# A fused two-block layer on one core: the y branch's units in halves of 256 features, with both parts of x in one moving operand

## The reference, cut to what matters

```python
h = rmsnorm(x, norm_mix_pre[l])
proj = h @ w_in[l]
xr, yr, q, k, v, g_rnn, g_attn = jnp.split(proj, IN_OFFSETS, axis=-1)
xr = causal_depthwise_conv(xr, conv_w[l], conv_b[l])
xr = rg_lru(xr, positions, w_rg_a[l], b_rg_a[l], w_rg_x[l], b_rg_x[l], lru_lambda[l])
y_rnn = xr * jax.nn.gelu(yr)
...
mix = jax.nn.sigmoid(g_rnn) * (y_rnn @ w_rnn_proj[l]) + jax.nn.sigmoid(g_attn) * (y_att @ w_attn_proj[l])
```

## Time and profile before

| | us |
|---|---|
| median of 3 runs | 2270.91 |
| lowest and highest | 2269.68 and 2271.86 |
| the profiled execution | 2270.5 |
| its span in the profile | 2268.8 |
| PE busy | 2250.7 (99% of the span) |
| DVE busy | 1420.2 (63%) |
| ACT busy | 1221.7 (54%) |
| POOL busy | 349.9 (15%) |

### The profile page before, as it was taken

How to read it: one execution, slowest core, us unless ns; L and a number is a source line. 1 busy time by engine, 2 the same in 40 slices (tenths; PEclk the granted TensorE clock), 3 DMA queues, 4 the chain that set the end, 5 groups by cost and what they waited for, 6 DMA issues and landing times.

```text
span 2268.8 us, 32847 instructions
## 1 busy us (share of the span) xinstructions
PE 2250.7 (99%) x11837; PEld 1896.5 (84%) x11837; DVE 1420.2 (63%) x1633; ACT 1221.7 (54%) x1915; POOL 349.9 (15%) x383
## 2 busy tenths in 40 slices
PE   9999999999999999999999999999999999999999
PEld 7888999888888888888888888889977778888887
DVE  6666656655454575555555555566899967765554
ACT  6666677544444456555555655555444446654443
POOL 2232210000000102121212112120333311110000
PEclk9999999999999999999999999999999999999999
DMA  7454454565555756566666666665556655555654
GB/s 240 151 168 149 148 180 145 195 194 192 192 190 194 244 193 211 197 208 196 203 205 199 201 203 201 195 208 180 177 182 195 191 172 171 166 161 187 192 187 167
DMA packets 215348, 427.10 MB, mean 188 GB/s; under 512 B 14096, under 2 KB 14384, under 8 KB 214960
## 3 DMA queue, kind: packets, MB, share of 16 engines
q1 hardware_dynamic: 206960, 398.57, 55.4%
q0 software_dynamic: 8048, 26.62, 3.8%
q10 hardware_dynamic: 208, 0.07, 0.0%
HBM read 414.71 MB, written 10.49 MB: 187 GB/s over the span
## 4 chain that ended last, share of the span: by engine, by line
PE 81%; DVE 12%; issue 3%; ACT 3%; POOL 1%; DMA 0%; DVEq 0%; ACTq 0%; SPq 0%
PE acc L1983 23%; PE acc L1985 23%; PE acc L1984 23%; DVE w_lo L1193 4%; PE acc L1975 3%; PE acc L1977 3%; PE acc L1978 3%; PE tps L1998 1%; ACT w_hi L674 1%; POOL k_t L589 1%; PE sides L2075 1%; POOL tmp L589 1%; PE tps L2093 1%; DVE slab_f_f L1755 1%; DVE k_t L1749 1%
## 5 line engine op out<-in xcount | busy, mean ns | idle before, releaser
L1193 DVE TENSOR_TENSOR w_lo<-raw,w_hi 128x1024 fp32r<-128x1024 f32 x752 | 942.8, 1258 | 752.4 <-ACT w_hi L674 748.3
L674 ACT ACTIVATE w_hi<-raw 128x1024 fp32r<-128x1024 f32 x752 | 794.7, 1059 | 848.9 <-PE acc L1985 733.4
L1983 PE MATMUL acc<-w_hi,h_hi 128*128 128x512 f32 x1440 | 571.5, 397 | 2.6 <-DVE w_lo L1193 1.7
L1985 PE MATMUL acc<-w_hi,h_lo 128*128 128x512 f32 x1440 | 561.8, 390 | 0.0
L1984 PE MATMUL acc<-w_lo,h_hi 128*128 128x512 f32 x1440 | 561.0, 390 | 0.0
L1983 PEld LDWEIGHTS acc<-w_hi,h_hi 128*128 128x128 f32 x1440 | 270.4, 188 | 68.2 <-issue 15.0
L1985 PEld LDWEIGHTS acc<-w_hi,h_lo 128*128 128x128 f32 x1440 | 270.3, 188 | 57.5
L1984 PEld LDWEIGHTS acc<-w_lo,h_hi 128*128 128x128 f32 x1440 | 270.8, 188 | 53.1
L1983 PE MATMUL acc<-w_hi,slab_dg_r 128*128 128x512 f32 x756 | 294.8, 390 | 0.0
L1985 PE MATMUL acc<-w_hi,slab_dg_r 128*128 128x512 f32 x756 | 294.3, 389 | 0.0
L1984 PE MATMUL acc<-w_lo,slab_dg_r 128*128 128x512 f32 x756 | 294.3, 389 | 0.0
(11 more groups left out here) (391 smaller groups left out, 2332.2 us busy)
## 6 DMA issues: line engine op xcount, KB each, us to landing
raw<-in_w_in_dram SPq DMA_DIRECT2D x328, 512.0 KB, 4.0
raw<-in_w_mlp_up_dram SPq DMA_DIRECT2D x128, 512.0 KB, 3.9
raw<-in_w_mlp_down_dram SPq DMA_DIRECT2D x128, 512.0 KB, 4.0
raw<-in_w_out_dram SPq DMA_DIRECT2D x64, 512.0 KB, 4.2
raw<-in_w_rnn_proj_dram SPq DMA_DIRECT2D x32, 512.0 KB, 3.8
raw<-in_w_attn_proj_dram SPq DMA_DIRECT2D x32, 512.0 KB, 3.8
trig_scratch<-tmp POOLq DMA_DIRECT2D x32, 256.0 KB, 3.8
raw<-in_w_proj_ssm_dram SPq DMA_DIRECT2D x16, 512.0 KB, 3.7
```

Source lines behind the costliest of these rows:

```text
L674: nc.scalar.activation(w_hi[:, j % RING], raw[:, j % RING], ACT.Copy).then_inc(hi_ready, 1)
L1193: V.tensor_tensor(w_lo[:, j % RING], raw[:, j % RING], w_hi[:, j % RING].bitcast(F32), ALU.subtract)\
L1983: T.matmul(o, hi[:, k, c], wh, start=first, stop=False)
L1985: ins = T.matmul(o, lo[:, k, c], wh, start=False, stop=last)
```

## The change

It touches the four y units only.

- SP loads, for each step, 4 k tiles by 256 columns in place of 2 k tiles by 512 (still 512 KB, in rows of 1 KB in place of 2 KB). Steps 0 to 3 of a unit make its first 256 features (half 0), steps 4 to 7 the second (half 1).
- `h_hi` and `h_lo` lie in one tensor `h_both`, so that one moving operand takes both: 256 columns of the high part and 256 of the low part. For each k tile and group of 128 features PE runs one matmul of 512 columns (stationary high weights) and one of 256 (stationary low weights), in place of three of 256.
- Half 0 uses `acc[1]`, half 1 `acc[0]`, in every unit. Each holds two sums per feature, a left one and a right one, which have to be added.
- Evacuation: ACT copies the right sums of a half (512 columns) into `yr_c` (`yr_right`); DVE adds the left sums and then multiplies by the row in a second instruction (`yr_half`, 2 of 512 columns). Half 0 is evacuated in the hooks of step 4 of its own unit, half 1 in the hooks of step 0 of the next.
- gelu moves on ACT from step 0 to step 1, ahead of the gates, and waits for the DVE instructions of half 1.

```diff
-                places = {0: [lambda: gelu(c)], 1: [lambda: gates(c)], 2: [lambda: decays(c)], 4: [lambda: root(c)]}
+                places = {0: [lambda: yr_right(c, 1)], 1: [lambda: gelu(c), lambda: gates(c)], 2: [lambda: decays(c)],
+                          4: [lambda: root(c)]}
...
+            def yr_right(c, h):
+                act.wait_ge(pe_used, (U_YR + c) * S + 4 * h + 4)
...
+                bank = acc[(U_YR + h) % 2][:, :].rearrange("p (m w c) -> p m w c", m=2, w=2)
+                nc.scalar.activation(yr_c[c % 2][:, 2 * h:2 * h + 2, :], bank[:, :, 1, :], ACT.Copy).then_inc(right_ready, 1)
...
+                hooks[4] = [lambda c=c: yr_right(c, 0)] + hooks.get(4, [])
...
+                return {0: [lambda: yr_half(c, 1)], 3: [lambda: decay(c)], 5: [lambda: states(c)], 6: [lambda: y_product(c)],
+                        7: [lambda: y_low(c)]}
+
+            def yr_half(c, h):
...
+                dve.wait_ge(right_ready, 2 * c + h + 1)
+                V.tensor_tensor(out_, left, out_, ALU.add).then_inc(done, 1)
+                dve.wait_ge(done, value)
+                V.tensor_tensor(out_, out_, row[:, :].unsqueeze(1).broadcast_to([P, 2, SEQ]), ALU.mult).then_inc(yr_ready, 1)
...
-                unit_over(None, 0, u * S)
-                rows_ = row[:, :].unsqueeze(1).broadcast_to([P, QPC, SEQ])
-                V.tensor_tensor(yr_c[c % 2], feat(acc[u % 2]), rows_, ALU.mult).then_inc(acc_free[u % 2], 1)
+                hooks = dict(beside_recurrence(c - 1) if c else beside_yr)
+                hooks[4] = hooks.get(4, []) + [lambda c=c: yr_half(c, 0)]
...
+                    for e in range(4):
+                        k = 4 * q + e
+                        for m in range(2):
+                            o = acc[par][:, m * NC:(m + 1) * NC]
+                            T.matmul(o.rearrange("p (w c) -> p w c", w=2), wh[:, e, m * P:(m + 1) * P], h_both[:, :, k, :],
+                                     start=k == 0, stop=False, skip_group_check=True)
+                            ins = T.matmul(o[:, 0:SEQ], wl[:, e, m * P:(m + 1) * P], h_hi[:, k, :], start=False, stop=k == KT - 1,
+                                           skip_group_check=True)
```

More of the change, by code:

```diff
@@ L116, in griffin_block_then_ssm_block @@
         w_lo = sb("w_lo", [P, RING, 2, NC], F32R)
-        h_hi = sb("h_hi", [P, KT, SEQ], F32R)
-        h_lo = sb("h_lo", [P, KT, SEQ], F32R)
+        h_both = sb("h_both", [P, 2, KT, SEQ], F32R)
+        h_hi, h_lo = h_both[:, 0, :, :], h_both[:, 1, :, :]
         slab_dg, slab_dgr = two_views("slab_dg", [P, 2 * KT, SEQ])
@@ L241, in griffin_block_then_ssm_block @@
         x_half_lo = sem("x_half_lo")
+        half_free, yr_ready = [sem(f"half_free{h}") for h in range(2)], sem("yr_ready")
+        right_ready = sem("right_ready")
         x_first, acc_half, sq_part = sem("x_first"), sem("acc_half"), sem("sq_part")
@@ L361, in griffin_block_then_ssm_block, with narrow @@
         row = t_low
+        def narrow(slot):
+            return slot.rearrange("p e (h n) -> p (e h) n", h=2)
         block = ctx.enter_context(nc.Block())
@@ L413, in _ @@
                 for j in range(2):
-                    unit(w_in, ds(past(i, 2 * NC, o_yr + j * NC), NC), past(i, 2 * S, (U_YR + j) * S))
+                    for s in range(S):
+                        sp.wait_ge(lo_ready, past(i, 2 * S, (U_YR + j) * S + s - LEAD))
+                        col = ds(past(i, 2 * NC, o_yr + j * NC + s // 4 * SEQ), SEQ)
+                        sp.dma_start(narrow(raw[:, s % RING, :, :]), w_in[s % 4 * 4 * P:(s % 4 + 1) * 4 * P, col]
+                                     .rearrange("(t p) n -> p t n", p=P)).then_inc(raw_landed[s % RING], 16)
             with sp.Fori(1, NH + 1) as i:
@@ L868, in gelu @@
             def gelu(c):
-                u = U_YR + c
-                act.wait_ge(acc_free[u % 2], u // 2 + 1)
+                act.wait_ge(yr_ready, 2 * c + 2)
                 nc.scalar.activation(yr_c[c % 2], yr_c[c % 2], ACT.Gelu_apprx_tanh).then_inc(gelu_ready, 1)
             def beside_recurrence(c):
-                places = {0: [lambda: gelu(c)], 1: [lambda: gates(c)], 2: [lambda: decays(c)], 4: [lambda: root(c)]}
+                places = {0: [lambda: yr_right(c, 1)], 1: [lambda: gelu(c), lambda: gates(c)], 2: [lambda: decays(c)],
+                          4: [lambda: root(c)]}
                 if c < NH - 1:
@@ L877, in beside_recurrence @@
                 return places
+            def yr_right(c, h):
+                act.wait_ge(pe_used, (U_YR + c) * S + 4 * h + 4)
+                if c == 0:
+                    act.wait_ge(tps_free, T_QX + NH)
+                if c > 1 and h == 0:
+                    act.wait_ge(y_ready, 2 * c - 2)
+                bank = acc[(U_YR + h) % 2][:, :].rearrange("p (m w c) -> p m w c", m=2, w=2)
+                nc.scalar.activation(yr_c[c % 2][:, 2 * h:2 * h + 2, :], bank[:, :, 1, :], ACT.Copy).then_inc(right_ready, 1)
             for c in range(NH):
-                u = U_YR + c
-                steps(None, 0, u * S, beside_recurrence(c - 1) if c else beside_yr)
+                hooks = dict(beside_recurrence(c - 1) if c else beside_yr)
+                hooks[4] = [lambda c=c: yr_right(c, 0)] + hooks.get(4, [])
+                steps(None, 0, (U_YR + c) * S, hooks)
             def mix_unit(i, c, n, hooks=None):
@@ L1470, in beside_recurrence @@
                 if c == NH - 1:
-                    return {3: [lambda: decay(c)], 5: [lambda: states(c)], 6: [lambda: scans(c)], 7: [lambda: y_product(c)]}
-                return {3: [lambda: decay(c)], 5: [lambda: states(c)], 6: [lambda: y_product(c)], 7: [lambda: y_low(c)]}
-            for c in range(NH):
[L1475 to L1478, removed]
-                unit_over(None, 0, u * S)
-                rows_ = row[:, :].unsqueeze(1).broadcast_to([P, QPC, SEQ])
-                V.tensor_tensor(yr_c[c % 2], feat(acc[u % 2]), rows_, ALU.mult).then_inc(acc_free[u % 2], 1)
+                    return {0: [lambda: yr_half(c, 1)], 3: [lambda: decay(c)], 5: [lambda: states(c)], 6: [lambda: scans(c)], 7: [lambda: y_product(c)]}
+                return {0: [lambda: yr_half(c, 1)], 3: [lambda: decay(c)], 5: [lambda: states(c)], 6: [lambda: y_product(c)],
+                        7: [lambda: y_low(c)]}
+            def yr_half(c, h):
+                par = (U_YR + h) % 2
+                out_ = yr_c[c % 2][:, 2 * h:2 * h + 2, :]
+                left = acc[par][:, :].rearrange("p (m w c) -> p m w c", m=2, w=2)[:, :, 0, :]
+                done, value = (half_free[h], c + 1) if c < 2 else (acc_free[par], (U_YR + h) // 2 + c - 1)
+                dve.wait_ge(right_ready, 2 * c + h + 1)
+                V.tensor_tensor(out_, left, out_, ALU.add).then_inc(done, 1)
+                dve.wait_ge(done, value)
+                V.tensor_tensor(out_, out_, row[:, :].unsqueeze(1).broadcast_to([P, 2, SEQ]), ALU.mult).then_inc(yr_ready, 1)
+            for c in range(NH):
+                hooks = dict(beside_recurrence(c - 1) if c else beside_yr)
+                hooks[4] = hooks.get(4, []) + [lambda c=c: yr_half(c, 0)]
+                steps(None, 0, (U_YR + c) * S, hooks)
             def mix_unit(i, c, n, hooks=None):
@@ L2129, in rg, with yr_unit @@
                 ins.then_inc(rg_done, 1)
+            def yr_unit(c, hooks):
+                for s in range(S):
+                    h, q = divmod(s, 4)
+                    par = (U_YR + h) % 2
+                    if q == 0:
+                        if c in (1, 2):
+                            pe.wait_ge(half_free[h], c)
+                        else:
+                            pe.wait_ge(acc_free[par], (U_YR + h) // 2 + c // 3)
+                    pe.wait_ge(lo_ready, (U_YR + c) * S + s + 1)
+                    wh, wl = narrow(w_hi[:, s % RING, :, :]), narrow(w_lo[:, s % RING, :, :])
+                    for e in range(4):
[6 more added lines that the diff above has]
+                                           skip_group_check=True)
+                        if e == 3:
+                            ins.then_inc(pe_used, 1)
+                        if e % 2:
+                            for f in hooks.get(2 * s + e // 2, []):
+                                f()
             for c in range(NH):
-                unit(None, 0, (U_YR + c) * S, 0, U_YR + c, h_hi, h_lo, by_feature=True,
-                     hooks={1: [lambda: rg(c - 1)]} if c else beside_yr)
+                yr_unit(c, {1: [lambda: rg(c - 1)]} if c else beside_yr)
             def mix_unit(i, c, n, hooks=None):
```

## The result

The changed kernel takes 2274.57 us (median; 2273.82 to 2276.52) beside 2270.72 for the kernel before in the same measurement (2269.17 to 2271.92): 3.85 us more, ratio 1.002 with a 95% interval of 1.0013 to 1.0026. The forecast was 2275.1, from a loop through ACT, DVE and gelu that grows from 29.94 to 31.61 us, three times.

The account below looks back on a forecast made before the run. A loop through ACT, DVE and gelu, as long as PE's, was taken to bind: 2270.5 + 5.0 − 0.8 = 2274.7, said as 2275.1 for the median. Forecast bounds were 2273.8 to 2276.6, the range 2271.5 to 2279.5.

Parts of the forecast that it names:

- The second loop: In the y units, a loop through ACT, DVE and gelu takes 29.94 us, as long as PE's, without room.
- The loop's new length: Gates on ACT in y2, y3 and the mix unit come 31.61 us apart, 1.67 more than before.
- A half costs DVE 1.32 us: Evacuating a half on DVE takes 0.71 + 0.61 us where other work follows, 1.42 up to gelu.
- ACT ties with DVE: Ahead of gelu, ACT's chain ends 30.6 us behind the gates and DVE's half 1 at 30.65.
- The pair saves 0.0133 us: On PE, matmuls of 512 and 256 columns take 0.3467 us, not 0.360; 0.85 us per unit, 3.4 in all.
- Gain ahead of the gates against three loops: PE gains 0.8 us ahead of y1's gates; three loops from there to the mix unit's gates lose 5.0.
- Transfers free: Weight loads in 1 KB rows take 1.55 to 3.1 us per step, under the step's 3.95, costing nothing.
- PE's waits: PE waits for low parts at steps 6 and 7 of y2, y3 and the mix unit, 7 to 8 us.
- The loop with room: Rival: ACT and DVE don't bind, so all of PE's 3.4 us gain comes through, 2267.5 us; 10%.
- The table load behind its wait: Rival: gelu's table load on ACT follows its wait, 1.28 us more in each of three loops, 2278.9; 10%.
- The transfers: Rival: weight loads over 3.95 us per step set the stage, about 10 us more, 2285; 6%.
- the alternation saves nothing: Rival: alternating matmul lengths saves PE nothing, so the 0.8 us is missing, 2275.9, inside the forecast's range.

Follow-up runs that it names:

- giving DVE 1.1 us: Changed kernel with half 1 evacuated at the end of its own unit's step 7 on ACT and DVE; 4.2 us over the kernel before, ratio 1.0019.
- the reordered kernel: Changed kernel with half 1 evacuated right behind the scans and gelu ahead of the high part of y; 2266.51 us beside 2269.99 for the kernel before.
- the 2 KB rows: Changed kernel with the y branch's weights loaded in rows of 2 KB again (wrong columns); 3.9 us over the kernel before, ratio 1.0016.
- the doubled low part: Kernel before, with DVE making one step's low part twice in each of y1, y2 and y3; 2.6 us more, ratio 1.0011.
- the one with the exchange in y0: Reordered kernel with ACT's right sums of half 0 copied behind the attention's copy in y0's step 4; 3.3 us under the kernel before, ratio 0.9986.

## Why the prediction was right, point by point

- *The second loop.* Right, and it is the case: shown from both sides, by the instruction added to the kernel before (+1.15 per loop at once) and by the order that takes gelu out of the tail (the gain comes through).
- *The loop's new length.* Predicted 31.61, measured 31.61 to 31.63. Its points, in us behind the gates at 327.07: product of y 24.61 predicted, 24.58 measured; low part 26.95, 26.92; next split 28.09, 28.06; half 1 29.23, 29.20; gelu 30.65, 30.65.
- *A half costs DVE 1.32 us.* Measured 1.32 (343.21 to 344.53). The Trainium skill, VectorE: DVE Perf Modes, section "The TRN2 errata — SBUF-src ops pay a fixed extra latency per instruction", has a large tile pay a fixed cost once where small ones pay it each time. The trace agrees: from the multiplication of 512 columns to the independent instruction behind it it is 0.60 us (343.93 to 344.53), twice that is 1.20, and 1024 columns take 1.14 (342.07 to 343.21).
- *ACT ties with DVE.* Right: giving DVE 1.1 us changed the loop by 0.07.
- *The pair saves 0.0133 us.* Right in y1 and y2 (0.3467 a pair, 0.85 a unit in the reordered kernel), and twice too much in y3 and in the larger part of y0 (0.3533 a pair, so 0.0067). In y0 the sum was mis-sized: 0.54 to 0.55 us on 72 pairs, 0.0076 each, where 0.96 was reckoned and 0.8 left after a wait. The wait that I put there for the attention's copy cost nothing: PE's weight load stands idle as long without it. The slower pace accounts for more than half of the missing 0.4 us, the first and last pairs of the stretches for the rest; why there are two paces stays open. In y3 the error cost the forecast nothing, as PE waits there anyway.
- *Gain ahead of the gates against three loops.* By the profiles +5.04 − 0.55 = +4.5; the sum said 5.0 − 0.8 = +4.2; the medians say +3.85, and the means of the same executions differ by 4.5. The ratio's interval, 3.0 to 5.9 us, holds them all. That the sum comes so near is in part luck: its second term was 0.25 too large.
- *The range.* Its lower bound of 1.45 a loop is not what its words give: with all four instructions at 0.61 the loop grows by 2 × 1.22 + 1.14 − 1.25 − 0.96 = 1.37. The measured 1.68 (94.85 less 89.81, by three) lies above both and under the upper bound of 1.9.
- *Transfers free.* Right, shown by the 2 KB rows and by the queue's unchanged share.
- *PE's waits.* 7 to 8 us predicted in six places, 7.9 measured on the weight loads, in six.
- *The rivals.* The loop with room fell with the doubled low part. The table load behind its wait fell: it starts at 356.35, before DVE's last multiplication. The transfers fell with the rows. That the alternation saves nothing fell with the pairs of 0.3467 us, in part only with those of 0.3533, where 0.360 is no saving. The price of 2.5 ns that the Trainium skill, TensorE: Matmul & The Clock Gate, section "Back-to-back issue gap", has for a matmul's start does not fit: beside 768 columns at 0.1067 us per 256, 0.3467 leaves 13 ns for each of the two starts.

The step that the range hung on was the choice to follow ACT and DVE, since PE had shown no wait.

## What to carry to other kernels

An engine that never waits may still have a neighbour loop exactly as long as its own; a saving on it then comes through only ahead of that loop, and any instruction added to the loop counts in full. Before shortening the busy engine's work, measure the distance between one landmark of the other engines from unit to unit, and see whether anything in that ring is idle. And where a strict order on an engine has a long idle spell before one late item (here 8.77 us before the high part of y), put the early items of the ring there: that turned a loss of 3.9 us into a gain of 3.5 by the medians (4.5 and 2.7 by the landmarks of the stage), with the same instructions.

## What was not expected of the hardware

The executions of the changed kernel go from 2273.8 to 2276.5 us, and the profiles of the two reordered kernels, which differ by one exchange on ACT, have spans of 2266.9 (the one with the exchange in y0) and 2264.6. Of these 2.3 us, 0.7 are there when y0 starts (256.69 and 255.98). By ACT's timelines the difference is still 0.6 at 1831 us, and it is 2.2 at 1838 us. These are the same stretch in both by the table of windows (us busy and count by engine, then the granted clock of PE), first the kernel with the exchange, then the reordered one:

```profile
1834.00:1860.00 26.00, 26.00 (x123) 20.73 (x116) 11.84 (x13) 10.25 (x12) 1.11 (x3) 0.93 0.60 185
```

```profile
1834.00:1860.00 26.00, 26.00 (x121) 21.23 (x114) 12.28 (x12) 11.00 (x13) 1.64 (x3) 1.00 0.67 202
```

In the first the mean granted clock is 0.93 over 26 us, which is a spell of some 3.6 us at the lower level, 1.2 GHz. In the 12 us ahead of it PE had been busy for 10.0 in either kernel. The reordered one had such a spell as well, between 1670 and 1700 us (0.94), and it cost less: the distance of the two timelines is 0.7 at 1660 us and again 0.7 at 1726. So a spell at the lower clock costs some 1.6 us in one place and nothing lasting in another. That this is also what spreads the executions of the changed kernel is likely and not shown: none of those above 2275 us has a mean granted clock of 1.000, but some of those below don't have it either (0.999). So small differences between medians here, such as 2.6 where the stage shows 3.45, or 3.85 where it shows 4.5, are better read from the stage's own landmarks.
